# gMLP's first operand taken from h before its norm, with the norm's factor moved to the results

## What is computed

```
    out = lax.map(block, (xb, ib, gb))                # peer_ffn: sum over the chosen experts
    ...
        h = h + peer_ffn(n2, ...).astype(h.dtype)
    return rmsnorm(h, norm_final_w).astype(x.dtype)   # end of the first block: norm "fin"
...
            m = gmlp_spatial_gating(rms_norm(h, g[0]), a_w_in[layer], ...)   # second block: norm "av"
...
def gmlp_spatial_gating(...):
    uv = jax.nn.gelu(h @ w_in)
    u, v = jnp.split(uv, 2, axis=-1)
    v = layer_norm(v, ln_g, ln_b)
    ...
    return (u * gate) @ w_out
        h = h + rms_norm(m, g[1])
```

## Time and profile before

| | us |
|---|---|
| median of three runs | 2666.98 (2665.46 to 2670.56) |
| the profiled execution, its own time | 2663.55 |
| its span, first to last instruction | 2661.8 |
| PE busy | 2610.0 (98%) |
| DVE busy | 1634.4 (61%) |
| ACT busy | 1077.1 (40%) |
| POOL busy | 997.1 (37%) |

### The profile page before, as it was taken

How to read it: one execution, slowest core, us unless ns; L and a number is a source line. 1 busy time by engine, 2 the same in 40 slices (tenths; PEclk the granted TensorE clock), 3 DMA queues, 4 the chain that set the end, 5 groups by cost and what they waited for, 6 DMA issues and landing times.

```text
span 2661.8 us, 37731 instructions
## 1 busy us (share of the span) xinstructions
PE 2610.0 (98%) x14486; PEld 2352.8 (88%) x14486; DVE 1634.4 (61%) x2997; ACT 1077.1 (40%) x1758; POOL 997.1 (37%) x546
## 2 busy tenths in 40 slices
PE   8999999999999999999999999999999999999998
PEld 6778899999999999999999888888889766988887
DVE  6754989888889878888888745610215265630112
ACT  5433344445555543333333434532323355442331
POOL 3323354544444433333333044344442413254442
PEclk9999999999999999999999999999999999999999
DMA  4323255689999989999999432233332321232331
GB/s 151 112 64 100 86 151 162 208 280 317 344 344 355 322 287 346 338 350 345 342 344 350 139 97 88 92 98 94 97 95 74 113 76 56 80 104 95 97 95 53
DMA packets 235473, 488.47 MB, mean 184 GB/s; under 512 B 85128, under 2 KB 135192, under 8 KB 235040
## 3 DMA queue, kind: packets, MB, share of 16 engines
q1 hardware_dynamic: 198432, 351.83, 41.3%
q0 software_dynamic: 36864, 134.23, 13.6%
HBM read 442.98 MB, written 42.88 MB: 183 GB/s over the span
## 4 chain that ended last, share of the span: by engine, by line
PE 93%; DVE 4%; ACT 1%; issue 1%; DMA 0%; POOL 0%; SPq 0%; DVEq 0%; ACTq 0%
PE ps L299 29%; PE ps L300 28%; PE ps L301 28%; PE ps L1707 3%; PE ps L483 1%; PE ps L2519 1%; PE ps L2607 1%; DVE tmpb L1101 1%; PE ps L1520 1%; DVE hT L2252 0%; PE ps L2571 0%; PE ps L529 0%; DVE wl L288 0%; DVE fo L2249 0%; ACT pt L2587 0%
## 5 line engine op out<-in xcount | busy, mean ns | idle before, releaser
L288 POOL TENSOR_TENSOR wl<-wraw,wh 128x1024 fp32r<-128x1024 f32 x253 | 616.3, 2442 | 1003.0 <-ACT wh L280 926.2
L280 ACT ACTIVATE wh<-wraw 128x1024 fp32r<-128x1024 f32 x487 | 513.7, 1058 | 1106.0 <-PE ps L301 1105.2
L299 PE MATMUL ps<-Xh,wh 128*128 128x384 f32 (+2 forms) x2336 | 861.9, 369 | 15.7 <-DVE wl L288 9.2
L300 PE MATMUL ps<-Xl,wh 128*128 128x384 f32 (+2 forms) x2336 | 821.0, 351 | 0.0
L301 PE MATMUL ps<-Xh,wl 128*128 128x384 f32 (+2 forms) x2336 | 819.6, 351 | 0.0
L299 PEld LDWEIGHTS ps<-Xh,wh 128*128 128x128 f32 x2336 | 442.5, 189 | 61.9 <-issue 17.7
L301 PEld LDWEIGHTS ps<-Xh,wl 128*128 128x128 f32 x2336 | 441.0, 189 | 39.2
L300 PEld LDWEIGHTS ps<-Xl,wh 128*128 128x128 f32 x2336 | 442.8, 190 | 36.3
L288 DVE TENSOR_TENSOR wl<-wraw,wh 128x1024 fp32r<-128x1024 f32 x234 | 286.2, 1224 | 137.1 <-ACT wh L280 136.9
L299 PE MATMUL ps<-Hh,wh 128*128 128x384 f32 x1024 | 344.8, 337 | 1.6 <-ACT gl L1762 1.6
L300 PE MATMUL ps<-Hl,wh 128*128 128x384 f32 x1024 | 344.1, 336 | 0.0
(11 more groups left out here) (304 smaller groups left out, 3297.6 us busy)
## 6 DMA issues: line engine op xcount, KB each, us to landing
wraw<-in_uT SPq DMA_DIRECT2D x128, 512.0 KB, 5.4
wraw<-in_v SPq DMA_DIRECT2D x128, 512.0 KB, 5.4
wraw<-in_up SPq DMA_DIRECT2D x128, 512.0 KB, 3.6
gA_scratch<-gl SPq DMA_DIRECT2D x122, 192.0 KB, 5.7
gl<-gA_scratch SPq DMA_DIRECT2D x122, 192.0 KB, 5.4
gG_scratch<-gbuf SPq DMA_DIRECT2D x64, 256.0 KB, 7.8
lg<-gG_scratch SPq DMA_DIRECT2D x128, 128.0 KB, 5.4
wraw<-in_w_q SPq DMA_DIRECT2D x24, 512.0 KB, 3.6
```

The costliest lines, as they stand in the source:

```text
L280: act.activation(wh[:, n % 4, :], wraw[:, n % 4, :], ACT.Copy).then_inc(s_wh, 1)
L288: pool.tensor_tensor(wl[:, n % 4, :], wraw[:, n % 4, :], wh[:, n % 4, :].bitcast(F32), ALU.subtract).then_inc(s_wl, 1)
L299: pe.matmul(o, ah, bh, start=start, stop=False)
L300: pe.matmul(o, ah, bl, start=False, stop=False)
```

## The change

The operand of gMLP's input projection is made from h as it stands after the expert output has been added, not yet normed: h times the product of both norms' weights (`fing`, made once by DVE). Both norms' factors then scale the projection's results: `both_roots_dve` multiplies the two. h itself is normed while PE runs the projection: the sums of the first norm and the spread of its factor stand between matmuls of the projection's chunks 1 and 2 (`fin_beside`). `va` and the folded identity are moved to the last three chunks of the memory that `Xl` uses, so that the low halves of chunks 0 to 4 can be written while they are still read. The low half of weight tile `A_V + 1` is made by POOL instead of DVE.

```diff
-    va = vat[:, 0:2, :].rearrange("p a t -> p (a t)")
-    foldI = vat[:, 2, 0:SP]
+    va = vat[:, 5:7, :].rearrange("p a t -> p (a t)")
+    foldI = vat[:, 7, 0:SP]
...
-        if n in (4, W_Q + 2, W_Q + 4, A_V + 4, F0 + 2, ...
+        if n in (4, W_Q + 2, W_Q + 4, A_V + 1, A_V + 2, A_V + 4, F0 + 2, ...
...
@@ pe_linear_tok
-            mm.then_inc(s_wuse, 1)
+                    if (k, tc) == (1, 3):
+                        mm.then_inc(s_wuse, 1)
+                    if (kc, tc) in beside:
+                        beside[kc, tc](pe)
...
+    def weight(w, i):
+        return fing[:, i:i + 1] if w == "fing" else col(w, i)
...
@@ down_act
         warm_sqrt(act)
+        act.wait_ge(s_fing, 1)
+        act.wait_ge(s_va, SP)
         for dc in range(8):
             act.wait_ge(s_hp, dc + 1)
             sum_square(act, "fin", dc, hT[:, dc, :])
+            if dc < 4:
+                fold_hi(act, "av", dc, "fing", 0)
+        for c in range(4, 8):
+            fold_hi(act, "av", c, "fing", 0)
+            if c == 4:
+                split_hi(act, A_V + 2)
         root_act(act, "fin", 5, 1.0 / 1024)
+        split_hi(act, A_V + 3)
...
@@ down_dve
+                dve.tensor_tensor(fing[:, :], vec[:, COLS["fin"]:COLS["fin"] + 8], vec[:, COLS["g2"]:COLS["g2"] + 8],
+                                  ALU.mult).then_inc(s_fing, 1)
...
             dve.tensor_tensor(hT[:, dc, :], hT[:, dc, :], ps[dc][:, :], ALU.add).then_inc(s_hp, 1)
-            if dc >= 2:
+            if dc == 1:
+                dve.wait_ge(s_fing, 1)
+                fold_lo(dve, "av", 0, "fing", 0)
+            if 2 <= dc < 7:
                 sum_add(dve, "fin", dc - 1)
+        fold_lo(dve, "av", 1, "fing", 0)
+        sum_add(dve, "fin", 6)
+        for c in range(2, 8):
+            fold_lo(dve, "av", c, "fing", 0)
+            if c == 3:
+                split_lo(dve, A_V + 2)
+            if c == 5:
+                root_dve(dve, "fin")
...
@@ down_pool
+        split_lo(pool, A_V + 1)
...
-    def fin_pe(pe):
-        root_pe(pe, "fin", 5)
-        spread_pe(pe, "fin", 6, (s_fin, 8))
+    def fin_beside():
+        beside = {(1, tc): (lambda pe, tc=tc: root_pe(pe, "fin", 5, at=tc)) for tc in range(4)}
+        beside[2, 2] = lambda pe: spread_pe(pe, "fin", 6, (s_fin, 8))
+        return beside
...
@@ fin_act
         for c in range(8):
             act.wait_ge(s_fin, c + 1)
-            fold_hi(act, "av", c, "g2", 0)
-            if c in (2, 4):
-                split_hi(act, A_V + 1 + c // 2)
-        for c in range(8):
             sum_square(act, "av", c, hT[:, c, :])
...
@@ fin_dve
-        root_dve(dve, "fin")
         dve.wait_ge(s_spr, a.spr + 1)
         for c in range(8):
             dve.scalar_tensor_tensor(out=hT[:, c, :], in0=hT[:, c, :], scalar=col("fin", c), in1=ps[6][:, :],
                                      op0=ALU.mult, op1=ALU.mult).then_inc(s_fin, 1)
-            if c:
-                fold_lo(dve, "av", c - 1, "g2", 0)
-            if c in (2, 4, 6):
-                split_lo(dve, A_V + c // 2)
-        fold_lo(dve, "av", 7, "g2", 0)
-        for c in range(1, 7):
-            sum_add(dve, "av", c)
+            if c == 1:
+                split_lo(dve, A_V + 3)
+            if c >= 2:
+                sum_add(dve, "av", c - 1)
+
+    def both_roots_dve(dve):
+
+        a = N["av"]
+        dve.wait_ge(s_root, a.i + 1)
+        dve.reciprocal(rst4[:, a.rs, :], rst4[:, a.rs, :]).then_inc(s_fing, 1)
+        dve.wait_ge(s_fing, 2)
+        dve.tensor_tensor(rst4[:, a.rs, :], rst4[:, a.rs, :], rst4[:, N["fin"].rs, :], ALU.mult).then_inc(s_rec, 1)
...
-        pe_linear_tok(pe, A_V, 0, B_TOK[0], XL["av"], lambda tc: (s_vn, tc + 1))
+        pe_linear_tok(pe, A_V, 0, B_TOK[0], XL["av"], lambda tc: (s_vn, tc + 1), beside=fin_beside())
...
-        root_dve(dve, "av")
+        both_roots_dve(dve)
...
-        fin_pe(pe)
```

More of the change, by code:

```diff
@@ L109, in build_program @@
     rst4 = sb("rst4", [128, 3, 4])
+    fing = sb("fing", [128, 8])
     ident = sb("ident", [128, 128])
@@ L284, in split_lo @@
             return
-        if n in (4, W_Q + 2, W_Q + 4, A_V + 4, F0 + 2, F0 + 4, W_K, W_K + 4, F1 + 2, F1 + 4) or n in U_TURNS:
+        if n in (4, W_Q + 2, W_Q + 4, A_V + 1, A_V + 2, A_V + 4, F0 + 2, F0 + 4, W_K, W_K + 4, F1 + 2, F1 + 4) or n in U_TURNS:
             pool.wait_ge(s_wl, n)
@@ L415, in last_halves, with pe_linear_tok @@
                 freed[b] = done(2 * hf + m)
-    def pe_linear_tok(pe, tile0, half, banks, x, done, each=None):
+    def pe_linear_tok(pe, tile0, half, banks, x, done, each=None, beside={}):
         for b in banks:
@@ L563, in x_lo @@
         e.tensor_tensor(Xl[:, c, :], src, Xh[:, c, :].bitcast(F32), ALU.subtract).then_inc(XL[name][c][0], 1)
+    def weight(w, i):
+        return fing[:, i:i + 1] if w == "fing" else col(w, i)
     def fold_hi(act, name, c, w, i0, hf=None):
         ts = slice(0, T) if hf is None else HALF[hf]
-        act.activation(Xh[:, c, ts], hT[:, c, ts], ACT.Identity, scale=col(w, i0 + c)).then_inc(s_xh, 1)
+        act.activation(Xh[:, c, ts], hT[:, c, ts], ACT.Identity, scale=weight(w, i0 + c)).then_inc(s_xh, 1)
     def fold_lo(dve, name, c, w, i0, hf=None):
@@ L572, in fold_lo @@
         dve.wait_ge(s_xh, XH[name][e])
-        dve.scalar_tensor_tensor(out=Xl[:, c, ts], in0=hT[:, c, ts], scalar=col(w, i0 + c), in1=Xh[:, c, ts].bitcast(F32),
+        dve.scalar_tensor_tensor(out=Xl[:, c, ts], in0=hT[:, c, ts], scalar=weight(w, i0 + c), in1=Xh[:, c, ts].bitcast(F32),
                                  op0=ALU.mult, op1=ALU.subtract).then_inc(XL[name][e][0], 1)
@@ L1933, in build_program @@
     s_vm, s_hp = sem("s_vm"), sem("s_hp")
+    s_fing = sem("s_fing")
     VADD = {}
```

## The result

The changed kernel takes 2650.76 us (median of four runs, 2648.64 to 2653.57) against 2667.72 us for the kernel before on the same chip (four runs, 2665.46 to 2670.56). The medians lie 17.0 us apart. The ratio is 0.9939, with a 95% interval of 0.9927 to 0.9950: 0.61% faster. The forecast was 2659.7 us, a gain of 7.3 us, with a range down to 2655: the sign was right, and the gain is more than twice what I worked out. The profiled execution took 2652.73 us (span 2650.9 us).

The account below looks back on a forecast made before the run. PE was taken as the bound, idle 8.07 us before the v projection. 8.07 less 2.7 of small matmuls plus 1.9 of slow clock gives 7.3 us, from 2666.98 to 2659.7 us; range 2655 to 2666.

Parts of the forecast that it names:

- The stream: gMLP's v projection on PE starts right after the expert output, small matmuls inside it: first half ends 7.3 us earlier.
- The slow-clock term: The v projection's first nine matmuls ran at 1.2 GHz, 0.21 us too long each; full clock gains 1.9 us.
- DVE has no room there: DVE's eight-chunk loop runs at 1.27 us per chunk, so the 0.7 us from added low half 0 is never made good.
- Margins of 0.3 and 0.4 us: Time by which low half 1 (0.3) and the last addition of squares (0.4) are ready before PE asks for them.
- Rival 1: DVE's low half 0 falls behind POOL's split or its queue slips; PE waits 2.1 us, gain 5.2 us; chance 0.12.
- Rivals 2 and 3: Projection start waits for chunk 7, gain 4.8 us (0.03); late second-half squares or splits, at the extreme all lost (0.09).
- Rival 4: Clock falls to 1.2 GHz in the projection's new stretch: 20 us more, less 7.3, 2680 us; chance 0.06 with anything like it.
- the cost of the new tile: Product of the two weights (128x8) with four more waits: a few tenths on DVE or ACT, before nothing PE waits for.

Follow-up runs that it names:

- e7: Changed kernel with the first norm's sums and spread put ahead of the projection again, operand, weights, scaling and addresses kept: 2658.68 us, ratio 0.9965 to the kernel before.
- e1: Kernel before with one unused tile of 32 bytes per partition after `rst4`, moving all later tiles: 2657.76 us, ratio 0.9962.
- e2: Kernel before with an unused tile of 64 bytes per partition after `rst4`, moving all later tiles: 2676.36 us, ratio 1.0032.
- e3: Kernel before with an unused tile of 96 bytes per partition after `rst4`, moving all later tiles: 2661.67 us, ratio 0.9976.
- e6: Kernel before with 64 unused bytes ahead of `Hh` and `Hl` alone: 2674.72 us, ratio 1.0024; twelve runs in two groups, 2664.5 to 2667.5 and 2673.8 to 2680.6 us.
- e9: Kernel before with 32 unused bytes ahead of `Fh` and 32 more ahead of `Fl`, nothing else moved: 2665.24 us.
- e12: Changed kernel with weight tile 1's low half made by DVE again, ahead of the eight additions to h, instead of POOL: 2650.40 us, ratio 0.9948 to the kernel before.
- e4: Changed kernel with 32 further unused bytes per partition after `rst4`, order untouched: 2668.84 us, ratio 1.0008 to the kernel before.
- e5: Changed kernel with `fing` placed behind other tiles so every earlier tile has its address of before: 2656.70 us, ratio 0.9961 to the kernel before.
- e8: Changed kernel with the second norm's sums also inside the stream and its root ahead of ACT's last split: 2649.54 us, ratio 0.9935 to the kernel before.
- e10: Changed kernel with `Xh` and `Xl` displaced to 32 past a multiple of 128 bytes, other operands on a multiple: 2671.84 us, ratio 1.0020 to the kernel before.
- e11: Changed kernel with `wh` and `wl` displaced to 32 past a multiple of 128 bytes, other operands on a multiple: 2686.66 us, ratio 1.0082 to the kernel before.

## Why the prediction was right about the order and wrong in its size

- **The stream: right.** 7.3 us forecast, 7.05 us in the trace, 7.0 and 7.5 us between medians at equal addresses, 7.9 us when the norm is put back in front (e7). The terms hold one by one: start 0.14 us after the last output matmul, sums at 0.45 us each, the spread at 0.90 us (1517.62 to 1518.43, and 0.09 behind it). The slow-clock term, taken from one profile, holds in all: the clock was 0.50 at the start of the v projection in all seven profiles with the first norm's sums in front (before, e1, e2, e3, e6, e7, e9), and 1.00 in all seven with them in the stream.
- **"DVE has no room there": wrong, and harmless.** The 1.27 us per chunk in the earlier trace rows was the pace at which PE delivered, read as DVE's own. Behind low half 0 DVE goes through an addition and a sum in 1.20 us (1502.70, 1503.90) and catches up: chunk 7 starts 0.72 us after PE's last output matmul, against 0.42 before and 1.1 forecast. Margins of 0.3 and 0.4 us were really 0.9 and 1.0. e12 loads the same queue with 1.2 us more, and PE still does not wait.
- **Rival 1, DVE late behind POOL: did not occur.** POOL's split began at 1499.42 and ended at 1501.82, before DVE's low half 0 began (1502.03). The collision shows elsewhere in the same trace, on the new 128x4 product of the reciprocals: it took 1.85 us and ended at 1537.07, when POOL went from its third split to its fourth (1536.99). The Trainium skill, "SBUF — State Buffer", section "Who interferes with whom", says that a DVE instruction with two SBUF inputs contends with a GpSimd instruction that reads SBUF; the trace agrees. Nothing on PE waited for the product.

```profile
1499.42 2.40 POOL L289 TENSOR_TENSOR wl<-wraw,wh 128x1024 fp32r<-128x1024 f32 x1 [37.94 <-ACT wh L281]
1529.97 9.41 POOL L289 TENSOR_TENSOR wl<-wraw,wh 128x1024 fp32r<-128x1024 f32 x4 [28.15 <-ACT wh L281]
```

```profile
1535.00 0.18 DVE L2093 RECIPROCAL rst<-rst 128x4 f32<-128x4 f32 x1 [6.19 <-ACT rst L521]
1535.22 1.85 DVE L2095 TENSOR_TENSOR rst<-rst 128x4 f32<-128x4 f32 x1
```

- **Rivals 2 and 3: did not occur.** The start was free, and the second half waited only 0.51 us for ACT's root, as before the change, not for a square or a split.
- **Rival 4, the slow clock: not where I put it.** It did not fall in the new stretch. It fell behind the second norm's sums in the profiled execution (1.65 us). Thirteen profiles have these sums in a row there: it fell in five (after, e1, e4, e5, e6) and stayed at 1.00 in eight, under either order. e12 differs from after in nothing that PE executes, and e1 from before in addresses alone. So neither the order nor the row of sums decides it; e8, with no row there, did not fall in its one profile.
- **The step that failed: the cost of the new tile.** The prediction prices the product of the weights ("128x8 ... a few tenths on DVE or ACT") and says nothing of where its 32 bytes lie. The product itself took 0.16 us of DVE; the bytes were the term that was put at nothing. They moved `Fh` and `Fl` from 96 past a multiple of 128 bytes onto one, and 1344 matmuls from 233.3 to 226.7 ns: 9.0 us by that count, some 8.7 us in the two traces, 10.1 us between medians when done alone (e1, interval 6.4 to 13.6). 7.05 and 8.7 make 15.8 us; the 1.2 us that remain to 17.0 are less than the measurement tells. It was not a term of my range either, and it has both signs: 32 bytes more, and the same change would have come out as no change (e4). That the gain came out as large as it did is luck. The trace of before showed it to whoever looked past the place of the change: matmuls of equal width at two spacings, 233.3 ns in the window of F and 226.7 ns in the earlier trace rows, PE busy and at full clock in both.

## What to carry to other kernels

An edit that adds or resizes a tile moves every tile declared behind it, and that can be worth more than the edit: list the addresses of the matmuls' operands, moving and stationary, before and after, try them on multiples of 128 bytes with padding (the best of the four places tried here), and give any change its control with equal addresses before its gain is put down to its order. Sums that a norm needs cost 0.45 us a pair inside a stream of matmuls and an idle gap with a slow clock in front of it; scaling results rather than the operand is what allows the move. An engine's pace in a profile is its own only where it does not wait; here it was its supplier's, and the queue had more room than the rows seemed to say.

## What the runs showed of the hardware

Mean time from start to start of fp32r matmuls at full clock, with PE busy throughout, by the operand's first byte in the partition after the last multiple of 128 (the other operand at 0). Each value is from one profile of a kernel; the 384-column ones leave out the seven longer steps around the matmuls on `va`:

| operand displaced | 512 columns | 384 columns |
|---|---|---|
| none (0) | 226.7 ns | 173.6 ns |
| moving, 64 | 228.9 (e3) | 173.6 (e3) |
| moving, 96 | 233.3 (before, e5) | 173.6 (before, e5) |
| moving, 32 | 233.3 (e2, e4), 234.3 (e10) | 176.9 (e2, e4), 173.6 (e6) |
| stationary, 32 | 233.3 (e11) | 176.9 (e11) |

Why the address matters is open: no run here looks inside the reads. Open too are the two groups of e6 (and with them whether the 176.9 ns at 32 past are owed to `Hh` and `Hl`), the mean of e9, and what decides in which executions the clock falls behind a norm's sums; each such fall cost 1.0 to 1.7 us. They are part of why runs of one kernel differ: of the 21 runs of before beside e1 to e4, the shortest (2663.61 us) had a mean clock of 0.996, and the three with 0.992 took 2669.09 to 2672.57 us.
